# An expert loop turned round: rows stationary and weights moving for experts 1 to 14, with three of eight chunks of gate and up in f32r passes

## The chip, the cores and the metric

The kernel runs on one core of one Trainium2 chip. The metric is the device time of one execution in microseconds. What is compared is the median of several runs.

## The reference, cut to what matters

One inference step of a one-layer encoder: 512 prompt rows and 64 sample rows of width 1024, first mixed (pooling and differential attention), then sent through a mixture of 16 experts of which each row uses two, then normalized. The part around the change is the mixture and the last norm:

```python
combine = jnp.sum(jax.nn.one_hot(expert_id, N_EXPERTS, dtype=jnp.float32) * top_w[..., None], axis=2)
moe = jnp.zeros((B, T, D_MODEL), jnp.float32)
for e in range(N_EXPERTS):
    he = jax.nn.silu(h2 @ w_gate[e]) * (h2 @ w_up[e])
    moe = moe + combine[..., e:e + 1] * (he @ w_down[e]).astype(jnp.float32)
x = x + moe.astype(x.dtype)
...
y_prompt = rmsnorm(xp, g_final)
y_sample = rmsnorm(xs, g_final)
```

Here h2 is T x 1024, w_gate and w_up are 1024 x 256 for each expert, and w_down is 256 x 1024. All data are float32.

## The kernel before, in words

Every engine has its own program, written out in order, and the engines meet at semaphores. Nothing reorders the work: what stands behind a waiting instruction on its engine waits too.

After the attention and the router, the loop over the 16 experts begins (the stages of the profile from 246 us on). Each expert has 128 slots for rows. The stage of expert i on TensorE is the function `expert` (line 1251): `gate_up` (line 1197) multiplies w_gate and w_up (stationary, eight chunks of 128 rows, two halves of 128 columns each) with the transposed rows xT (moving, 128 columns), 32 products in f32, each of which the profile lists as two matmul instructions. Then `transpose_rows` turns the next expert's gathered rows, `slot_lists` makes the lists of rows for expert i+3, and `down_split` (line 1212) makes the down product of expert i-1 in three f32r passes: each f32 operand is split into a high part (he_hi, w_hi) and a low part (he_lo, w_lo), and high x high, high x low and low x high are summed. Since the hidden values come out of gate and up transposed already, they go straight into the down product.

In an iteration i ScalarE (lines 1590 to 1640) takes the square sum of a finished row block (`square_sum`, from i = 6 on), then `silu(i)`, then eight copies with a scale of the next expert's transposed rows from PSUM to xT (`rows_out`), then `wd_his(i+1)`: the two casts that make the high part of the next expert's w_down. VectorE (lines 2136 to 2230) makes he, he again and its low part (`he_out`), the lists (`lists_out`), a one-hot matrix, the norm of a finished row block (`finish_row`, from i = 6 on), the accumulation of expert i-1's result (`add_rows`), and the low part of w_down (`wd_los`).

The weights of an expert are three loads of 1 MB (w_gate, w_up, w_down) that SyncE issues into a ring of four slots, all with one semaphore a slot (`ring_loaded`, 48 when the three are there). The gate and up loads of expert i+4 go out when gate and up of expert i are done. The w_down load of expert i+3 goes out when the down product of expert i-1 is done, that is at the end of stage i, and when a gather of rows has landed (line 560). GpSimd issues, for each expert, the gather of its h2 rows (line 702), the gather of their sums so far, the store of sums, and from expert 6 on the two stores of finished rows (line 707). The store of sums waits for the accumulation.

Of the kernel before, what the change touches and what calls it, by code (L numbers as in the profile page):

```python
# [34 lines left out]
P = 128  # L35
# [26 lines left out]
RING = 4  # L62
NOWHERE = 1024
# [24 lines left out]
def build(nc, x_prompt, x_sample, cache_k, cache_v, state_pool, g_mix, w_in, w_pool, pool_scale,  # L88
# [4 lines left out]
    with ctx:  # L93
# [65 lines left out]
        region_v = sb("region_v", [P, 3584])  # L159
# [30 lines left out]
        def wd_hi(i):  # L190
            return wd_hi_last if isinstance(i, int) and i == E - 1 else wd_hi_two[:, i % 2]
        wd_lo = [r.rearrange("p (c n) -> p c n", c=FC) for r in
# [18 lines left out]
        hT_pair = w_hi_extra[:, :].rearrange("p (k b t) -> p k b t", k=KC, b=2)  # L211
        w_out_hi = [region_p_r[:, 0:D], region_p_r[:, D:2 * D], region_x_r[:, 0:D], region_x_r[:, D:2 * D], ring0_r[:, 4096:5120], ring0_r[:, 5120:6144],
# [94 lines left out]
        gsub_loaded = sem("gsub_loaded")  # L307
# [14 lines left out]
        gfin_loaded = sem("gfin_loaded")  # L322
# [22 lines left out]
        hist_full = sem("hist_full")  # L345
        hist_evac = sem("hist_evac")
        lam_dots = sem("lam_dots")
        lam_exp = sem("lam_exp")
        lam_made = sem("lam_made")
# [42 lines left out]
        early_onehot = sem("early_onehot")  # L392
        oh_last_ready = sem("oh_last_ready")
# [10 lines left out]
        he_lo_ready = sem("he_lo_ready")  # L404
        wd_hi_ready = sem("wd_hi_ready")
# [15 lines left out]
        ov_w_free = sem("ov_w_free")  # L421
        ov_gather_begun = sem("ov_gather_begun")
# [9 lines left out]
        last_bias = sem("last_bias")  # L432
# [22 lines left out]
        def _(sp):  # L455
# [51 lines left out]
            sp.dma_start(gsub[:, :], g_subln.rearrange("a (v o) -> (a v) o", o=1)).then_inc(gsub_loaded, 16)  # L507
# [47 lines left out]
            for i in range(E - RING):  # L555
# [6 lines left out]
                if i == 2:  # L562
                    sp.wait_ge(routed, 1)
                    sp.dma_start(gfin, g_final.rearrange("(a d) -> a d", a=1).to_broadcast([P, D])).then_inc(gfin_loaded, 16)
# [5 lines left out]
            with sp.If(n_ov > 0):  # L570
                with sp.Fori(0, MAXOV) as j:
                    with sp.If(j < n_ov):
                        e = sp.value_load(ctl[0:1, DS(j, 1)], min_val=0, max_val=E - 1)
                        load_expert(RING - 1, e, ov_w_loaded)
                        sp.wait_ge(ov_down_done, j + 1)
                        sp.sem_inc(ov_w_free, 1)
# [11 lines left out]
        def _(pool):  # L588
# [50 lines left out]
            pool.wait_ge(lam_made, 1)  # L639
# [107 lines left out]

            gather_first()
# [11 lines left out]
            for i in range(E):  # L760
# [10 lines left out]
                if 1 <= i < E - 1:  # L771
                    gather_acc(i + 1)

# [10 lines left out]
            with pool.If(n_ov > 0):  # L784
# [8 lines left out]
                with pool.Fori(0, MAXOV) as j:  # L793
                    with pool.If(j < n_ov):
                        pool.wait_ge(ov_idx_ready, j + 1)
                        pool.sem_inc(ov_gather_begun, 1)
# [3 lines left out]
                        pool.sem_inc(ov_gather_begun, 1)  # L800
                        store_acc(0, ov_stored)
                        pool.wait_ge(ov_final, j + 1)
                        pool.sem_inc(ov_gather_begun, 1)
# [9 lines left out]
        def _(pe):  # L813
# [124 lines left out]
            ins.then_inc(hist_full, 1)  # L938
# [8 lines left out]
            pe.wait_ge(hist_evac, 1)  # L947
# [212 lines left out]
            pe.wait_ge(early_onehot, 1)  # L1160
# [51 lines left out]
            def down_split(u, i, bank):  # L1212

                b, w_hi = u % 2, wd_hi(i if isinstance(i, int) else u)
                for half in range(2):
# [8 lines left out]
                    ins.then_inc(down_done, 1)  # L1224

            def first_rows():
# [6 lines left out]
                pe.wait_ge(oh_last_ready, 1)  # L1233
# [17 lines left out]
            def expert(it, u, left):  # L1251
# [5 lines left out]
                def lists_of(n):  # L1257
                    pe.wait_ge(onehot_ready, i + n + 1)
                    pe.wait_ge(idx_ready, i + n + EARLY + (1 if first and n == 0 else 0))
                    slot_lists((u + n) % RING * EPG + it + (u + n) // RING, (u + n) % RING)  # L1260
# [3 lines left out]
                pe.wait_ge(xT_act, i + 1)  # L1264
                pe.wait_ge(ring_loaded[u], it * 48 + 48)
                gate_up(u, b, up_full)
# [12 lines left out]
                if not first and left != 0:  # L1279
                    if isinstance(it, int) and i == 1:  # L1280
                        pe.wait_ge(state_evac, 1)
                    pe.wait_ge(he_ready, i)
                    if not (isinstance(it, int) and i == 1):
                        pe.wait_ge(added, i - 1)
                    pe.wait_ge(wd_lo_ready, i)
                    down_split((u - 1) % RING, i - 1, 4)
                if left == 1:
                    pe.wait_ge(idx_ready, E + EARLY + 1)
                    pe.wait_ge(he_ready, i + 1)
# [22 lines left out]
            pe.wait_ge(xT_act, E)  # L1312
# [20 lines left out]
        def _(act):  # L1333
# [88 lines left out]
            act.wait_ge(lam_dots, 1)  # L1422
# [184 lines left out]

            act.wait_ge(h2T_dve, NT)
            wd_his(0)

# [11 lines left out]
            for i in range(E):  # L1622
# [5 lines left out]
                if i + 1 < E:  # L1628
                    act.wait_ge(xg_transposed, i + 2)
                    for k in range(4 if i == 0 else 0, KC):  # L1630
# [710 lines left out]
```

## Time and profile before

| | |
|---|---|
| median of 3 runs | 435.69 us (435.27 to 435.9) |
| the profiled execution | 435.72 us, its span 433.6 us |
| mean granted clock of TensorE | 0.994 of full speed |
| TensorE busy | 413.9 us, 95% of the span |
| VectorE busy | 273.2 us, 63% |
| ScalarE busy | 197.8 us, 46% |
| GpSimd busy | 126.3 us, 29% |
| stages of experts 8 to 12 | 10.98 to 11.0 us each |

The span is the stretch from the first to the last instruction; the time of an execution is some 2.1 us longer. A matmul instruction is listed with the time from its start to its modelled end, so neighbours overlap: what a product costs in a stream is read from start to start, or from the chain, where its pieces stand end to end.

### The profile page before, as it was taken

The numbers are of one execution on the slowest core, as the hardware profiler recorded it, in microseconds if no ns is written. First come the engines' busy times: TensorE is split into PE (matmuls) and PEld (weight loads), VectorE is DVE, ScalarE is ACT, GpSimd is POOL, SyncE is SP. The second block draws the span as 40 slices with busy tenths as digits, with TensorE's granted clock in tenths as the row PEclk, the third lists the DMA queues.
The fourth block names the chain that finished last, engine by engine and source line by source line (L and its number), as shares of the span: only waits on it lengthen the run. The fifth ranks groups of instructions, "written<-read, shape, count | busy, mean of one in ns | idle before, by whom it ended". The sixth has DMA issues, their size and how long they took to land.

```text
span 433.6 us, 7776 instructions
## 1 busy us (share of the span) xinstructions
PE 413.9 (95%) x2919; PEld 364.1 (84%) x2919; DVE 273.2 (63%) x655; ACT 197.8 (46%) x485; POOL 126.3 (29%) x209
## 2 busy tenths in 40 slices
PE   6899999999999999999999999999989999999991
PEld 3687999997876886788887799999989999999981
DVE  2756430805759898635346898755566777776974
ACT  5566230705565766332222734444544555555632
POOL 2012000200034325151000323333334555554443
PEclk9999999999999999999999999999999999999997
DMA  7951704406000049923223789899999989986121
GB/s 250 323 182 50 231 2 135 169 2 202 2 1 3 0 155 418 373 97 147 97 98 129 245 322 421 335 403 379 355 339 341 374 332 386 364 321 251 59 89 47
DMA packets 32073, 91.36 MB, mean 211 GB/s; under 512 B 11200, under 2 KB 11712, under 8 KB 27942
## 3 DMA queue, kind: packets, MB, share of 16 engines
q1 hardware_dynamic: 20790, 71.97, 44.4%
q0 software_dynamic: 11248, 18.93, 12.3%
q8 instruction: 21, 0.34, 0.4%
q14 instruction: 14, 0.11, 0.1%
HBM read 86.38 MB, written 26.01 MB: 259 GB/s over the span
## 4 chain that ended last, share of the span: by engine, by line
PE 78%; DMA 7%; DVE 6%; ACT 4%; issue 3%; POOL 0%; SPq 0%; DVEq 0%; ACTq 0%; POOLq 0%
PE ps L1201 23%; PE ps L829 10%; PE ps L831 9%; PE ps L830 9%; DMA region_w<-in_w_down 5%; PE ps L1218 3%; PE ps L1219 3%; PE ps L1223 3%; PE ps L1194 3%; PE ps L993 2%; PE ps L1135 2%; PE ps L958 2%; DMA region_x<-in_x_prompt 1%; PE ps L976 1%; PE ps L1122 1%
## 5 line engine op out<-in xcount | busy, mean ns | idle before, releaser
L1201 PEld LDWEIGHTS ps<-region_p,region_a 128*128 128x128 f32 x512 | 58.3, 192 | 1.0 <-DVE region_p L2042 0.4
L1201 PE MATMUL ps<-region_p,region_a 128*128 128x128 f32 x512 | 58.5, 275 | 0.0
L831 PE MATMUL ps<-region_a_r,region_w_r 128*128 128x288 f32 x192 | 56.5, 295 | 0.0
L829 PE MATMUL ps<-region_a_r,ring_r 128*128 128x288 f32 x128 | 40.6, 317 | 0.0
L830 PE MATMUL ps<-region_a_r,ring_r 128*128 128x288 f32 x128 | 37.7, 295 | 0.0
L831 PEld LDWEIGHTS ps<-region_a_r,region_w_r 128*128 128x128 f32 x192 | 36.0, 188 | 0.0
L1592 ACT ACTIVATE region_p<-ps,gffn_sb 128x128 f32<-128x128 f32 x116 | 31.6, 384 | 7.7 <-PE ps L1194 7.7
L1613 ACT ACTIVATE region_t<-ps 128x256 f32<-128x256 f32 x16 | 6.1, 384 | 57.8 <-PE ps L1201 57.8
L1201 PEld LDWEIGHTS ps<-region_p,region_w 128*128 128x128 f32 x256 | 29.1, 192 | 1.8 <-issue 1.6
L702 POOL DMA_INDIRECT region_x<-h_rows,lists x13 | 16.7, 1283 | 47.3 <-DVE slot_w L2145 47.3
L1201 PE MATMUL ps<-region_p,region_w 128*128 128x128 f32 x256 | 29.3, 275 | 1.2 <-DMA region_w<-in_w_down 1.2
L829 PEld LDWEIGHTS ps<-region_a_r,ring_r 128*128 128x128 f32 x128 | 24.1, 188 | 6.8 <-issue 3.3
L1201 PEld LDWEIGHTS ps<-region_p,ring 128*128 128x128 f32 x256 | 29.1, 192 | 0.8 <-DVE region_p L2064 0.5
L1201 PE MATMUL ps<-region_p,ring 128*128 128x128 f32 x256 | 29.3, 276 | 0.4 <-DVE region_p L2064 0.4
L2151 DVE TENSOR_TENSOR region_t_r<-region_t,ps 128x256 fp32r<-128x256 f32 x16 | 6.7, 418 | 33.7 <-ACT region_t L1613 33.7
L2168 DVE SCALAR_TENSOR_TENSOR mix<-ps,slot_w,mix 128x1024 f32<-128x1024 f32 x15 | 19.2, 1281 | 10.6 <-PE ps L1223 6.3
L1783 DVE TENSOR_SCALAR region_q<-ps 128x288 f32<-128x288 f32 x8 | 3.7, 457 | 34.0 <-PE ps L831 34.0
L830 PE MATMUL ps<-region_w_r,mix_r 128*128 128x512 f32 x64 | 25.0, 391 | 0.0
L1218 PE MATMUL ps<-region_q_r,region_t_r 128*128 128x512 f32 x60 | 24.7, 411 | 0.0
L830 PEld LDWEIGHTS ps<-region_a_r,ring_r 128*128 128x128 f32 x128 | 24.1, 188 | 0.0
L1453 ACT ACTIVATE region_p<-ps,negm 128x128 f32<-128x128 f32 (+4 forms) x40 | 20.8, 528 | 5.8 <-DVE negm L1815 5.8
L707 POOL DMA_INDIRECT out_y_prompt<-region_x,lists x12 | 12.0, 1004 | 34.1 <-DVE region_x L2184 31.0
(365 smaller groups left out, 1020.1 us busy)
## 6 DMA issues: line engine op xcount, KB each, us to landing
region_a<-in_w_gate SPq DMA_DIRECT2D x8, 1024.0 KB, 9.3
region_a<-in_w_up SPq DMA_DIRECT2D x8, 1024.0 KB, 17.5
region_a<-in_w_down SPq DMA_DIRECT2D x8, 1024.0 KB, 18.5
region_w<-in_w_in SPq DMA_DIRECT2D x2, 2048.0 KB, 10.1
region_w<-in_w_out SPq DMA_DIRECT2D x2, 2048.0 KB, 7.9
ring<-in_w_gate SPq DMA_DIRECT2D x4, 1024.0 KB, 8.6
ring<-in_w_up SPq DMA_DIRECT2D x4, 1024.0 KB, 17.2
ring<-in_w_down SPq DMA_DIRECT2D x4, 1024.0 KB, 13.2
```

The costliest lines, as they stand in the source:

```text
L702: pool.indirect_dma_start(out=dst, out_offset=None, in_=src, in_offset=bass.IndirectOffsetOnAxis(ap=at, axis=0), bounds_check=bound[n], oo ...
L829: pe.matmul(out, lhs_hi, rhs_hi, start=first, stop=False)
L830: pe.matmul(out, lhs_hi, rhs_lo, start=False, stop=False)
L831: return pe.matmul(out, lhs_lo, rhs_hi, start=False, stop=last)
L1194: ins = pe.transpose(ps[:, k // 4, (k % 4) * P:(k % 4 + 1) * P], src[:, k, :], ident[:, :])
L1201: ins = pe.matmul(ps[:, 2 + b, (first + c) * P:(first + c + 1) * P], w[:, k, c * P:(c + 1) * P], xT[:, b, k, :], start=(k == 0), stop=(k = ...
L1218: pe.matmul(ps[:, bank + half, :], he_hi[:, b, c, :], w_hi[:, c, n], start=(c == 0), stop=False)
L1219: pe.matmul(ps[:, bank + half, :], he_hi[:, b, c, :], wd_lo[u][:, c, n], start=False, stop=False)
L1223: ins = pe.matmul(ps[:, bank + half, :], he_lo[:, b, c, :], w_hi[:, c, n], start=False, stop=(c == FC - 1))
L1453: ins = act.activation(prob[0:m, n % 2, c, 0:w], ps[0:m, 2 * (n % 2) + c, 0:w], ACT.Exp, bias=negm[0:m, n % 2, c:c + 1], scale=-1.0, accum ...
L1592: return act.activation(xT[:, b, k, :], ps[:, k // 4, (k % 4) * P:(k % 4 + 1) * P], ACT.Copy, scale=gffn_sb[:, k:k + 1])
L2168: dve.scalar_tensor_tensor(acc, ps[:, bank:bank + 2, :], slot_w[:, w:w + 1], acc, ALU.mult, ALU.add).then_inc(added, 1)
```

## The change

For experts 1 to 14 the rows become the stationary operand of gate and up, and the weights of w_gate and w_up (256 columns side by side) the moving one (`gate_up_mixed`). Five of the eight chunks stay in f32, ten products. The other three are made in three f32r passes, 18 products, for which both operands are split: the high parts of the rows come from ScalarE (`rows_hi`) and their low parts from VectorE (`rows_lo`); the high parts of the first three chunks of both weights come from ScalarE (`gu_his`, two tiles of 768 columns) and the low parts from VectorE (`gu_los`). The hidden values now come out with the rows on the partitions, so TensorE transposes them (`transpose_he`, two transposes between the halves of the down product of the expert before), and ScalarE and VectorE read the high and low parts from PSUM. GpSimd takes over one of the two halves of the low part of w_down for experts 1 to 13 (`wd_lo_half`). With POOL_FROM at 768, GpSimd has no part of the other subtraction. The one-hot matrix moves behind the norm of a finished row block on VectorE, the overflow counts two iterations later, and the load of the final gain two experts later. Some semaphores are merged.

```diff
+NF = 3
+POOL_FROM = 768
...
+            def gate_up_mixed(slot, b, i, signal):
+
+                hi, lo = wgu_hi[slot % 2], wgu_lo[slot]
+                for a in range(2):
+                    out = ps[:, 2 + b, a * FE:(a + 1) * FE]
+                    for k in range(NF, KC):
+                        pe.matmul(out, xT[:, b, k, :], wgu_sb[slot][:, a, k], start=(k == NF), stop=False)
+                    if a == 0:
+                        pe.wait_ge(xlo_ready, i)
+                        pe.wait_ge(gu_lo_ready, i)
...
+                    for k in range(NF):
+                        f = slice(k * FE, (k + 1) * FE)
+                        ins = three_passes(out, xT_hi[:, b, k, :], xT_lo[:, b, k, :], hi[a][:, f], lo[a][:, f], False, k == NF - 1)
+                ins.then_inc(signal, 1)
...
+            def transpose_he(u, i):
+
+                pe.wait_ge(he_ready, i + 1)
+                for c in range(FC):
+                    ins = pe.transpose(ps[:, 6 + u % 2, FE + c * P:FE + (c + 1) * P], he_tok[:, u % 2, c * P:(c + 1) * P], ident[:, :])
+                ins.then_inc(heT_full, 1)
...
+            def gu_his(i):
+
+                act.wait_ge(ring_loaded[i % RING], 48 * (i // RING + 1))
+                if i >= 2:
+                    act.wait_ge(up_full, i - 1)
+                for a in range(2):
+                    act.copy(wgu_hi[i % 2][a], wgu_part[i % RING][a]).then_inc(gu_hi_ready, 1)
...
+            def rows_hi(i):
+
+                b = i % 2
+                for k in range(NF, 4):
+                    rows_out(b, k)
+                for k in range(NF):
+                    ins = act.activation(xT_hi[:, b, k, :], ps[:, 0, k * P:(k + 1) * P], ACT.Copy, scale=gffn_sb[:, k:k + 1])
+                ins.then_inc(xhi_ready, 1)
...
+                    if mixed(i):
+                        he_hi_out(i)
                     if i < E - 2:
                         wd_his(i + 1)
                     if i == E - 3:
                         wd_his(E - 1)
+                    if mixed(i + 2):
+                        gu_his(i + 2)
...
+            def rows_lo(i):
+
+                b = i % 2
+                dve.wait_ge(xhi_ready, i)
+                for k in range(NF):
+                    ins = dve.scalar_tensor_tensor(xT_lo[:, b, k, :], ps[:, 0, k * P:(k + 1) * P], gffn_sb[:, k:k + 1],
+                                                   xT_hi[:, b, k, :].bitcast(F32), ALU.mult, ALU.subtract)
+                ins.then_inc(xlo_ready, 1)
...
+            def wd_lo_half(i):
+
+                pool.wait_ge(wd_hi_ready, FC * i + 2)
+                pool.tensor_tensor(wd_lo[i % RING][:, 1, :], wd_sb[i % RING][:, 1, :], wd_hi(i)[:, 1, :].bitcast(F32),
+                                   ALU.subtract).then_inc(lo_by_pool, 1)
...
                 elif i + EARLY < E:
                     lists_out(i + EARLY)
+                if i >= 1 and mixed(i + 1):
+                    rows_lo(i + 1)
+                if mixed(i):
+                    he_lo_out(i)
+                if i > RING + 1:
+                    finish_row(i - 2)
                 if i + EARLY + 1 < E:
                     expert_onehot(i + EARLY + 1)
-                if i > RING + 1:
-                    finish_row(i - 2)
                 if i >= 1:
                     add_rows(i - 1)
                 if i < E - 2:
                     wd_los(i + 1)
                 if i == E - 3:
                     wd_los(E - 1)
+                if mixed(i + 2):
+                    gu_los(i + 2)
```

On ScalarE, the order of one iteration before (the one in which expert 11's silu, L1613, is made and expert 12's w_down is cast from `ring`):

```order
L1619 ACTIVATE region_q,ssq<-mix 128x1024
L1613 ACTIVATE region_t<-ps 128x256
L1592 ACTIVATE region_p<-ps,gffn_sb 128x128 x8
L1606 CAST region_q_r<-ring 128x1024 x2
L1619 ACTIVATE region_q,ssq<-mix 128x1024
```

The same iteration of the change (L1713 is the square sum, L1707 the silu, L1694 the high parts of the rows, L1699 the high part of he, L1683 the high parts of gate and up):

```order
L1713 ACTIVATE region_q,ssq<-mix 128x1024
L1707 ACTIVATE region_t<-ps 128x256
L1661 ACTIVATE region_p<-ps,gffn_sb 128x128
L1694 ACTIVATE region_p_r<-ps,gffn_sb 128x128 x3
L1661 ACTIVATE region_p<-ps,gffn_sb 128x128 x4
L1699 CAST region_t_r<-ps 128x256
L1675 CAST region_q_r<-ring 128x1024 x2
L1683 CAST region_w_r<-region_a 128x768 x2
L1713 ACTIVATE region_q,ssq<-mix 128x1024
```

The two casts of 768 columns read the slot (`region_a`) of expert 13, two experts on, and stand ahead of the next square sum and silu.

On TensorE, the end of gate and up and the down product before (expert 12's stage; L1201 is gate and up, L1194 the transposes of rows, L1218 to L1223 the down product's passes):

```order
L1201 MATMUL ps<-region_p,ring 128x128 x32
L1194 MATMUL ps<-ident,region_x 128x128 x8
L1188 MATMUL ps<-region_q,region_v 128x8 x5
L1218 MATMUL ps<-region_q_r,region_t_r 128x512
L1219 MATMUL ps<-region_w_r,region_t_r 128x512
```

The change at the stage of expert 13: one f32 group and the first f32r products (L1246 is f32, L857 to L859 the three passes):

```order
L1246 MATMUL ps<-region_a,region_p 128x256 x5
L857 MATMUL ps<-region_w_r,region_p_r 128x256
L858 MATMUL ps<-region_a_r,region_p_r 128x256
L859 MATMUL ps<-region_w_r,w_hi_extra 128x256
L857 MATMUL ps<-region_w_r,region_p_r 128x256
```

One group of five f32 products and nine f32r products is made for gate, and one for up. Behind the first half of the down product two transposes (L1261) are new.

## Rows read from the trace of the kernel before

**Rows 1.** The page, busy time and the chain's shares by engine
```profile
PE 413.9 (95%) x2919; PEld 364.1 (84%) x2919; DVE 273.2 (63%) x655; ACT 197.8 (46%) x485; POOL 126.3 (29%) x209
...
PE 78%; DMA 7%; DVE 6%; ACT 4%; issue 3%; POOL 0%; SPq 0%; DVEq 0%; ACTq 0%; POOLq 0%
```
**Rows 2.** Chain of waits, expert 7's weights, then expert 10's stage: start, us, what
```profile
300.06 23.00 DMA region_w<-in_w_down
...
356.37 7.14 PE ps L1201 x64
363.51 0.87 PE ps L1194 x8
...
366.89 0.45 PE ps L1223 x2
```
**Rows 3.** Windows, stages of experts 1, 6, 10, 14: busy, clock, DMA share, GB/s
```profile
255.64:267.07 11.43, 11.43 (x102) 10.94 (x102) 9.59 (x37) 4.30 (x11) 2.32 (x2) 1.00 1.01 408
...
311.04:323.20 12.16, 10.95 (x89) 10.12 (x89) 7.82 (x19) 5.71 (x14) 4.10 (x3) 1.00 0.94 345
...
356.37:367.35 10.98, 10.98 (x91) 10.47 (x91) 8.27 (x19) 5.71 (x13) 5.97 (x5) 1.00 0.97 385
...
400.18:411.84 11.66, 11.66 (x89) 11.03 (x89) 10.63 (x19) 7.50 (x15) 4.62 (x3) 1.00 0.22 70
```
**Rows 4.** Issues of w_down (experts 7, 8, 14), and their us to landing
```profile
300.06 0.38 SPq L485 DMA_DIRECT2D region_w<-in_w_down  x1
...
311.04 0.38 SPq L485 DMA_DIRECT2D ring<-in_w_down  x1
...
383.76 0.38 SPq L485 DMA_DIRECT2D region_a<-in_w_down  x1
...
region_w<-in_w_down SPq DMA_DIRECT2D x1, 1024.0 KB, 23.0
...
ring<-in_w_down SPq DMA_DIRECT2D x1, 1024.0 KB, 22.1
...
region_a<-in_w_down SPq DMA_DIRECT2D x1, 1024.0 KB, 11.1
```
**Rows 5.** Chain: f32 products of 288 columns; timeline: f32r ones, first and last
```profile
171.18 0.97 PE ps L1029 x4
...
49.72 0.29 PE L829 MATMUL ps<-region_a_r,ring_r 128*128 128x288 f32 x1
...
53.95 0.30 PE L831 MATMUL ps<-region_a_r,region_w_r 128*128 128x288 f32 x1
```
**Rows 6.** ScalarE's groups from 334.4 to 367.4, three iterations
```profile
L1592 ACT ACTIVATE region_p<-ps,gffn_sb 128x128 f32<-128x128 f32 x24 | 6.5, 385 | 1.5 <-PE ps L1194 1.5
L1606 ACT CAST region_q_r<-region_a 128x1024 fp32r<-128x1024 f32 x4 | 4.0, 1044 | 1.7 <-PE ps L1223 1.7
L1619 ACT ACTIVATE region_q<-mix 128x1024 f32<-128x1024 f32 x3 | 3.2, 1057 | 2.7 <-DVE mix L2168 2.7
```
**Rows 7.** VectorE's groups of the same stretch; GpSimd's 1024-wide memset of the span
```profile
L2158 DVE TENSOR_TENSOR region_a_r<-region_a,region_q_r 128x1024 fp32r<-128x1024 f32 x4 | 4.7, 1218 | 0.0
...
L2151 DVE TENSOR_TENSOR region_t_r<-region_t,ps 128x256 fp32r<-128x256 f32 x3 | 1.3, 421 | 7.2 <-ACT region_t L1613 7.2
...
L678 POOL MEMSET region_x<- 128x1024 f32 x1 | 1.3, 1268 | 0.0
```
**Rows 8.** Late gathers: issues, us to landing, and VectorE's wait
```profile
373.88 1.03 POOL L702 DMA_INDIRECT mix<-summed_rows,lists  x1 [0.30 <-issue]
...
376.63 1.34 POOL L702 DMA_INDIRECT region_x<-h_rows,lists  x1 [1.73 <-DVE slot_w L2145]
...
mix<-summed_rows,lists POOLq DMA_INDIRECT x1, 19.7
...
region_x<-h_rows,lists POOLq DMA_INDIRECT x1, 19.7
...
393.68 1.28 DVE L2168 SCALAR_TENSOR_TENSOR mix<-ps,slot_w,mix 128x1024 f32<-128x1024 f32 x1 [3.21 <-DMA mix<-summed_rows,lists]
```

More of the change, by code:

```diff
@@ L404, in build @@
         he_lo_ready = sem("he_lo_ready")
+        heT_full = sem("heT_full")
+        heT_hi = sem("heT_hi")
+        gu_hi_ready = sem("gu_hi_ready")
+        gu_lo_ready = sem("gu_lo_ready")
+        lo_by_pool = sem("lo_by_pool")
+        xhi_ready = sem("xhi_ready")
+        xlo_ready = sem("xlo_ready")
         wd_hi_ready = sem("wd_hi_ready")
@@ L772, in _ @@
                     gather_acc(i + 1)
+                if 1 <= i + 1 <= E - 3:
+                    wd_lo_half(i + 1)
+                if POOL_FROM < NF * FE and 3 <= i + 2 < E - 1:
+                    gu_lo_part(i + 2)
             pool.wait_ge(routed, 1)
@@ L946, in _ @@
             pe.wait_ge(ktok_evac, NT)
[L947 removed]
+            pe.wait_ge(ktok_evac, NT + 1)
             def scores(n):
@@ L1224, in down_split @@
                     ins.then_inc(down_done, 1)
+                    if half == 0 and between is not None:
+                        between()
             def first_rows():
@@ L1259, in lists_of @@
                     pe.wait_ge(idx_ready, i + n + EARLY + (1 if first and n == 0 else 0))
+                    if n == EARLY and not (isinstance(it, int) and i <= 1):
+                        pe.wait_ge(he_lo_ready, i)
                     slot_lists((u + n) % RING * EPG + it + (u + n) // RING, (u + n) % RING)
@@ L1263, in expert @@
                     pe.wait_ge(xT_dve, i + 1)
-                pe.wait_ge(xT_act, i + 1)
+                pe.wait_ge(xT_act, i + 1 if first else i)
                 pe.wait_ge(ring_loaded[u], it * 48 + 48)
-                gate_up(u, b, up_full)
+                if isinstance(it, int) and i == 1:
+                    pe.wait_ge(xhi_ready, 1)
+                if first or left == 0:
+                    gate_up(u, b, up_full)
+                else:
+                    gate_up_mixed(u, b, i, up_full)
                 if isinstance(it, int) and i == 1:
@@ L1629, in _ @@
                     act.wait_ge(xg_transposed, i + 2)
-                    for k in range(4 if i == 0 else 0, KC):
-                        ins = rows_out((i + 1) % 2, k)
-                    ins.then_inc(xT_act, 1)
+                    if mixed(i + 1):
+                        rows_hi(i + 1)
+                    if i >= 1:
+                        for k in range(4 if mixed(i + 1) else 0, KC):
+                            ins = rows_out((i + 1) % 2, k)
+                        ins.then_inc(xT_act, 1)
+                    if mixed(i):
+                        he_hi_out(i)
                     if i < E - 2:
```

138 lines of the change are left out of this document (91 added, 47 removed).

## The prediction

> **What bounds the kernel now.** I read the page first: TensorE is busy for 413.9 of 433.6 us and holds 78% of the chain that ended last [rows 1]. A reader would stop there and count matmuls. The stages say more. In the chain of waits, a stage of one expert takes 10.98 us (from 356.37 to 367.35): 7.14 for the gate and up product, then 3.84 for eight transposes, the lists and twelve down products [rows 2]. But in the same rows one stage waits for a weight load: w_down, issued at 300.06, arrives 23.00 later. So I read the stages' windows and the loads. The DMA share is 1.01, 0.94 and 0.97 in three stages of the loop, and 0.22 in expert 14's [rows 3]. And w_down of expert 7 is issued at 300.06 and lands 23.0 later, at 323.06; that of expert 8 goes out at 311.04, 12 us before, and lands at 333.14; that of expert 14 goes out at 383.76 and lands at 394.86 [rows 4]. Each is issued before its forerunner has landed, so the queue never runs dry: six experts' loads land in 394.86-333.14 = 61.7 us, 10.29 each, at the pace of the transfers and not at that of TensorE. Call this D. TensorE's 10.98 is longer, which is why it waits once only: the loads gain 0.7 us a stage on it.
>
> **The change, part by part.** I write S(i) for the start of expert i's stage and measure from the profiled execution: span 433.6, time 435.72, which is 0.03 from the median 435.69.
>
> *Gate and up.* Removed: 32 f32 products of 128 columns, 7.14 us. Added: 10 f32 products of 256 columns. The four instructions of two f32 products of 288 columns take 0.97 [rows 5], 0.485 a product, or 0.431 at 256: 4.31. And 18 f32r products of 256 columns: 33 of 288 columns start from 49.72 to 53.95 [rows 5], 0.132 each, so 0.117 at 256: 2.11. Sum 6.42, less 0.72. A denser pace from fewer columns could be eaten by weight loading for every product; but there is a load for every product now too, 2919 and 2919 [rows 1], so I take the sum (bounds 6.2, and 6.7 with f32r left at 0.132). Added too: two transposes at 0.87/8 = 0.11 [rows 2], 0.22. The rest of a stage becomes 4.06. Net 0.50 a stage, P = 10.48. If TensorE decided all 14 stages: -7.0 us.
>
> *The high parts of the weights.* ScalarE now casts two tiles of 768 for expert j in the iteration of j-2, and it waits there for all three loads of j; before, the first use was the cast of w_down at the end of j-1's stage. These casts stand ahead of the square sum and of the silu of j-1 on the same queue. Prices: 1024 wide is 1.00 (4.0 for 4), so 2 x 0.75 = 1.50; the square is 1.06 plus its 0.19 read, 1.25; a silu is like 0.38, eight row copies take 6.5/3 = 2.2 [rows 6]. The silu of j-1 can start at S(j-1)+6.42. How late may it be? The down products take 0.45 for two [rows 2], so their second half starts 1.37 before the stage's end, at 2.47 after gate and up, and he must be there: silu 0.38, product 0.42 [rows 7], hand-overs about 0.2, so 1.4 us of slack; by the row copies 4.06-0.4-2.2 = 1.4 as well; VectorE leaves about 1.0 (below). I take 1.2. So the loads of j must have landed by S(j-1)+6.42+1.2-1.25-1.50 = S(j-1)+4.9. Before it was S(j-1)+10.98 or so: 6 us later.
>
> *What the loads then allow.* The final gain (0.5 MB, about 1.7 us at D for 3 MB) moves behind expert 7's loads, so they land at 321.4 and S(6) >= 316.5; TensorE alone would have been there at 311.04-5x0.50 = 308.5, plus up to 2 for stage 1, where the two subtractions (2x0.92) stand behind expert 0's work: swallowed by this wait. S(7) >= 333.14-4.9 = 328.2, against 323.2 before. By then fewer gathers have used the queue: moved are 385 GB/s x 10.98 = 4.2 MB a stage [rows 3] of which weights are 3.15, so a quarter is gathers and stores; the landing now falls 0.45 of a stage earlier in that work, 0.45 x 0.25 x 10.29 = 1.2; I take 1.0: S(7) = 327.2. From there P (10.48) is over D (10.29), and TensorE decides: S(14) = 327.2+7x10.48 = 400.6, against 400.18: **+0.4**.
>
> *VectorE and the order of its work.* Busy 8.27 in the stage of expert 10 [rows 3]. Less one product of 256 (0.42) and one subtraction of 1024 (1.18, from 4.7 for 4), plus three 128-wide low parts (0.22 to 0.42 each, I take 0.25) and two subtractions of 768 (0.92): 9.3 of 10.48. It is still covered, but in a queue: the low part of he can't start before 3.65 after gate and up (8 row copies and a cast on ScalarE stand ahead), and 8.3 us follow it, the norm of a finished row (3.0), the one-hot (0.8), the accumulation (1.2), 1.2 and 1.8. It ends 1.5 into the next expert, where 2.0 is what TensorE allows. So an accumulation ends at 9.0 after gate and up, where before it was 6.7, and GpSimd's store and gather of sums behind it go out about 1 us later. Behind them GpSimd gets half of the w_down subtraction: nearest rows a 1024-wide memset 1.27 [rows 7] and two such operands at most twice that, 1.3 to 2.5. The gather of h2 rows behind it goes out about 1 us later. One-hots behind the norm cost nothing by themselves.
>
> *The gathers.* They were on the edge already: the sums for expert 11, whose gather was issued at 373.88, land 19.7 later, and VectorE waited 3.21 for them, covered then; the h2 rows for expert 14, issued at 376.63, landed 19.7 later, at 396.3 [rows 8], and were wanted at the end of gate and up of expert 13, 367.35+2x10.98+7.14 = 396.45. Now two stages are 1.0 shorter and the issue is 1.0 later: 1.9 late on TensorE, and VectorE's wait is no longer covered, at about the same place. I take **+1.8** once (bounds 0 and 4). Stage 14: -0.50, and +0.5 for VectorE's low parts of the last two w_down, which are not halved: 0.
>
> Sum 0.4+1.8+0 = **+2.2**, so 435.72+2.2 = 437.9.
>
> [...] The stage of expert 10 moved 385 GB/s, and that of expert 1 408 [rows 3]. [...]
>
> **Rivals.**
> - *Forecast*, loads and gathers cost more than TensorE gains: +1 to +4.5. 0.42.
> - *Loads are no limit*: the queue serves faster when asked earlier, TensorE decides. For it: DMA share 0.94 and 0.97, not 1, in two of the stages. Against: the landings above. 14x0.50 less 1.5 for stage 1: -5.5, 430.2. This ends on the other side. 0.12.
> - *The two sides cancel*: weights land 2 us earlier, or the gathers still fit. 435 to 436.5, 436.0. 0.30, a third of it more than 0.2% faster.
> - *VectorE becomes the bound*: its subtractions read two tiles from SBUF, and GpSimd's subtraction runs beside them. From 0.5 us of extra a stage it decides. With 1.27 lost a stage, 0.8 over eight stages: +6, 442. [...] 0.16.
>
> **How the numbers follow.** What a measurement of this kernel can tell is 0.2%, 0.9 us. Faster: 0.12+0.10 = 0.22. Same: 0.20. Slower: 0.42+0.16 = 0.58. The range leaves out the first rival and the tail of the last: 433.0 to 443.0. The forecast's own range is 436.7 to 440.2.
>
> **What would show it.** Right: gate and up in 6.3 to 6.6 us; quiet stages of 10.5; TensorE waiting around experts 5 to 7, with ScalarE's casts of 768 ended by a w_down load; expert 7's loads landing at 320 to 323 in spite of earlier stages; stage 14 starting at 401 to 404; a late wait for gathered rows. Wrong: weights that land 3 us or more earlier (then I am 3 to 7 too high); gate and up at 6.9 or more; stages over 11 with VectorE without idle time (then too low).

## The result and the profile after

| | before | after |
|---|---|---|
| median of 4 runs each | 435.79 us (435.27 to 436.96) | 445.63 us (445.54 to 447.16) |
| ratio, 95% interval | 1 | 1.0219 [1.0187, 1.0251] |
| span of the profiled execution | 433.6 us | 443.7 us |
| granted clock of TensorE | 0.994 | 0.990 |

The change costs 2.2%, about 9.5 us (the interval excludes 1, and not 1.02). The direction was forecast; the size, 437.9 us in a range up to 443, was not. All ratios, here and below, leave out the few executions in which the granted clock stood far lower (0.65 to 0.85 on average, 462 us and more). They are those on record, each against the kernel before on its chip, and differ somewhat from the quotients of the medians: for e1 below, 1.0106 beside 440.78/437.25 = 1.0081. The first rows of the page of the changed kernel answer to [rows 1]: busy time, the chain's shares by engine, and one group of instructions (count, busy us, mean ns, idle time before).

```profile
PE 412.0 (93%) x2583; PEld 350.5 (79%) x2583; DVE 309.2 (70%) x698; ACT 221.8 (50%) x527; POOL 162.8 (37%) x222
...
PE 53%; DVE 27%; issue 6%; DMA 6%; ACT 6%; POOL 0%; SPq 0%; DVEq 0%; ACTq 0%; POOLq 0%
...
L2311 DVE SCALAR_TENSOR_TENSOR root<-root 128x1 f32<-128x1 f32 x33 | 22.7, 688 | 1.2
```

TensorE lost hardly any busy time, and the chain moved from TensorE (78% before, 53% now) to VectorE (6%, now 27%). The group is the strangest row of the page: an operation on one element in each partition takes 688 ns on average. TensorE's own part came out as worked out. The chain of waits in the stage of expert 6:

```profile
317.26 2.16 PE ps L1246 x10
319.42 0.12 PE ps L857
...
320.49 2.16 PE ps L1246 x10
...
323.72 0.87 PE ps L1222 x8
...
326.18 0.22 PE ps L1261 x2
...
327.79 0.86 PE ps L1246 x4
```

Ten f32 instructions (five products) take 2.16 us, an f32r product 0.12; gate and up take 323.72-317.26 = 6.46, and a stage with nothing in its way 327.79-317.26 = 10.53. The forecast had 6.42 and 10.48. The windows of two such stages and of two late ones answer to [rows 3] (length, busy us of PE, PEld, DVE, ACT, POOL with counts, clock, DMA share, GB/s):

```profile
263.62:274.18 10.56, 10.56 (x71) 9.48 (x68) 7.39 (x16) 6.21 (x14) 8.09 (x6) 1.00 0.87 347
317.26:327.79 10.53, 10.53 (x67) 9.44 (x66) 6.86 (x15) 7.33 (x16) 6.73 (x4) 1.00 0.94 361
355.65:367.49 11.84, 10.74 (x67) 9.36 (x66) 11.56 (x23) 7.32 (x16) 9.21 (x7) 1.00 0.91 328
404.10:414.10 10.00, 9.47 (x53) 8.13 (x52) 9.56 (x19) 6.69 (x15) 6.37 (x5) 1.00 0.18 49
```

The late stage takes 11.84, and VectorE is busy for 11.56 of it. The timeline there shows why (start, us, engine, line):

```profile
361.01 2.58 DVE L2311 SCALAR_TENSOR_TENSOR root<-root 128x1 f32<-128x1 f32 x1
361.19 2.38 POOL L762 TENSOR_TENSOR region_a_r<-region_a,region_q_r 128x1024 fp32r<-128x1024 f32 x1
...
363.83 0.22 DVE L2311 SCALAR_TENSOR_TENSOR root<-root 128x1 f32<-128x1 f32 x1
```

VectorE's tiny operation with two inputs from SBUF takes 0.22 us when it is alone and 2.58 when it meets GpSimd's subtraction, and it ends 0.02 after it. VectorE stands still for 2.36 us, nearly the whole of GpSimd's 2.38. It happens again at 372.85, 384.67, 396.49 and 407.57 (and before, at 349.18), 2.57 to 2.59 each time.

The second place is the stage of expert 3. The chain of waits there:

```profile
264.44 9.01 DMA region_x<-h_rows,lists
273.51 8.93 DMA ring<-in_w_down
282.46 0.84 ACT region_v_r L1683
283.32 4.21 DVE ring_r L2281 x2
...
290.97 0.25 DVE region_k L2220
291.25 0.43 DVE region_t L2253
```

The gather of h2 rows holds SyncE until 273.5, w_down of expert 4 goes out behind it and lands at 282.4, and the casts of its gate and up wait for it. Then the two subtractions take 4.21 where two alone take 1.83 (again beside GpSimd), and the overflow count, which the change put here, follows until 291.2 before VectorE comes to the hidden values for which TensorE waits. TensorE stands for 4.4 us, until 291.72. Something comes on top that no line of the chain names: toward the end of that stop the granted clock of TensorE goes down to 0.50 and stays there for 3.35 us. The windows of that stretch and of the whole interval:

```profile
291.22:294.57 3.35, 2.85 (x8) 2.37 (x9) 2.56 (x8) 0.37 (x1) 1.01 (x1) 0.50 0.73 300
284.69:301.17 16.48, 12.06 (x67) 10.43 (x66) 14.35 (x33) 6.39 (x14) 6.52 (x5) 0.90 0.83 322
```

TensorE works for 2.85 of these 3.35 us, at half its pace (down products 0.43 from start to start, where those before the stop have 0.23), so some 1.4 us are lost. The 5.95 us by which this interval is over the 10.53 of a quiet one therefore part into 2.38 beside GpSimd (4.21 less 1.83), 1.4 at half clock, and 2.2 for the late load and the count; e1 below, without the other two, has 1.9 for these. In the next interval (11.86) GpSimd meets the placing of the overflow: an operation of 0.24 takes 2.62. Here are the intervals between the ends of gate and up of neighbouring experts, read in each trace from the start of the eight transposes of rows behind them. "Tail" is the rest of the span after expert 14.

| kernel | 1 | 2 | 3 | 4 | 5 to 7 | 8 | 9 to 13, sum | 14 (last) | sum of 14 | tail |
|---|---|---|---|---|---|---|---|---|---|---|
| before | 9.79 | 10.98 | 10.98 | 11.01 | 10.97, 10.98, 12.43 | 10.97 | 54.95 | 10.82 | 153.88 | 26.44 |
| after | 10.76 | 10.56 | 10.51 | 16.48 | 11.86, 10.52, 10.53 | 10.53 | 58.36 | 11.07 | 161.18 | 29.66 |
| e1 | 10.76 | 10.56 | 10.53 | 12.40 | 10.51, 10.52, 10.53 | 13.23 | 55.85 | 10.32 | 155.21 | 27.85 |
| e5 | 10.76 | 10.56 | 10.51 | 11.71 | 10.54, 10.52, 10.53 | 10.86 | 58.85 | 10.51 | 155.35 | 27.75 |
| e6 | 10.76 | 15.54 | 10.50 | 10.51 | 10.54, 10.53, 10.53 | 13.04 | 55.88 | 10.32 | 158.15 | 27.84 |
| e9 | 10.75 | 10.57 | 10.53 | 11.68 | 10.53, 10.52, 10.53 | 10.86 | 53.37 | 10.33 | 149.67 | 27.82 |
| e10 | 9.79 | 11.04 | 10.97 | 11.01 | 10.98, 10.98, 10.98 | 10.98 | 54.90 | 10.75 | 152.38 | 26.38 |
| e11 | 10.75 | 10.56 | 10.54 | 15.15 | 11.51, 10.53, 10.52 | 10.53 | 58.37 | 11.09 | 159.55 | 29.65 |

Interval k ends with gate and up of expert k, so a wait in the second part of expert 3's stage stands in column 4, and one in expert 7's in column 8. Each row is one profiled execution. Some of them hold stretches at half clock, which other executions of the same kernel may lack: 1.4 to 1.7 us lost in column 4 of the change and of e11, in column 2 of e6, and in the interval 13 of e5 (12.16, mean clock 0.86). The loops of before and e1 ran at 1.00 throughout.

### The profile page after: what moved, and what is told of

The parts are those of the page before. It is cut to its first block, busy times and chain, and to the rows that moved or that the text cites. A ratio compares the mean times of both kernels' runs of the same rounds, so it can differ in the third digit from the quotient of the medians.

```text
span 443.7 us, 7253 instructions
## 1 busy us (share of the span) xinstructions
PE 412.0 (93%) x2583; PEld 350.5 (79%) x2583; DVE 309.2 (70%) x698; ACT 221.8 (50%) x527; POOL 162.8 (37%) x222
## 4 chain that ended last, share of the span: by engine, by line
PE 53%; DVE 27%; issue 6%; DMA 6%; ACT 6%; POOL 0%; SPq 0%; DVEq 0%; ACTq 0%; POOLq 0%
PE ps L857 10%; PE ps L859 9%; PE ps L858 9%; DVE root L2311 5%; PE ps L1246 3%; DVE region_a_r L2281 2%; DVE mix L2301 2%; PE ps L1021 2%; DMA region_x<-h_rows,lists 2%; DMA ring<-in_w_down 2%; PE ps L1163 2%; PE ps L1229 2%; PE ps L986 2%; DMA region_x<-in_x_prompt 1%; DVE ring_r L2281 1%
## 5 line engine op out<-in xcount | busy, mean ns | idle before, releaser
L859 PE MATMUL ps<-region_a_r,region_w_r 128*128 128x288 f32 x192 | 56.6, 295 | 0.0
L857 PE MATMUL ps<-region_a_r,ring_r 128*128 128x288 f32 x128 | 40.6, 317 | 0.0
L1246 PE MATMUL ps<-region_a,region_p 128*128 128x256 f32 x160 | 37.2, 380 | 0.0
L859 PEld LDWEIGHTS ps<-region_a_r,region_w_r 128*128 128x128 f32 x192 | 36.1, 188 | 0.0
L1246 PEld LDWEIGHTS ps<-region_a,region_p 128*128 128x128 f32 x160 | 29.8, 190 | 4.3 <-DVE region_p L2143 0.5
L857 PEld LDWEIGHTS ps<-region_a_r,ring_r 128*128 128x128 f32 x128 | 24.1, 188 | 6.8 <-issue 3.3
L1713 ACT ACTIVATE region_q<-mix 128x1024 f32<-128x1024 f32 x11 | 11.7, 1060 | 27.5 <-DVE mix L2301 27.5
L1661 ACT ACTIVATE region_p<-ps,gffn_sb 128x128 f32<-128x128 f32 x74 | 22.4, 391 | 4.2 <-PE ps L1222 4.2
L718 POOL DMA_INDIRECT summed_rows<-mix,lists x12 | 18.0, 1503 | 15.3 <-DVE mix L2301 13.2
L2311 DVE SCALAR_TENSOR_TENSOR root<-root 128x1 f32<-128x1 f32 x33 | 22.7, 688 | 1.2
L713 POOL DMA_INDIRECT region_x<-h_rows,lists x13 | 13.6, 1046 | 24.8 <-DVE slot_w L2246 23.3
L1617 ACT ACTIVATE region_v<-region_q 128x512 f32<-128x512 f32 (+1 forms) x10 | 6.3, 627 | 32.0 <-DVE region_q L2023 21.8
L718 POOL DMA_INDIRECT out_y_sample<-region_x,lists x12 | 19.1, 1589 | 3.7 <-issue 3.7
L2023 DVE TENSOR_TENSOR region_q<-ps,region_q 128x512 f32<-128x512 f32 (+1 forms) x10 | 6.8, 685 | 18.8 <-PE ps L859 18.2
```

What stands on the lines that cost most here:

```text
L713: pool.indirect_dma_start(out=dst, out_offset=None, in_=src, in_offset=bass.IndirectOffsetOnAxis(ap=at, axis=0), bounds_check=bound[n], oo ...
L718: pool.indirect_dma_start(out=dst, out_offset=bass.IndirectOffsetOnAxis(ap=at, axis=0), in_=src, in_offset=None, bounds_check=bound[n], oo ...
L857: pe.matmul(out, lhs_hi, rhs_hi, start=first, stop=False)
L859: return pe.matmul(out, lhs_lo, rhs_hi, start=False, stop=last)
L1246: pe.matmul(out, xT[:, b, k, :], wgu_sb[slot][:, a, k], start=(k == NF), stop=False)
L1661: return act.activation(xT[:, b, k, :], ps[:, k // 4, (k % 4) * P:(k % 4 + 1) * P], ACT.Copy, scale=gffn_sb[:, k:k + 1])
```

## The experiments

Theory A is the stop: GpSimd's subtraction (2.38) holds VectorE's operations with two inputs from SBUF, and VectorE then sets the stage. Theory B is the forecast's: loads and gathers take back what TensorE gains. The rivals to both are the moved overflow count and the order of the one-hot.

**e1, VectorE makes both halves.**

```diff
-                if 1 <= i + 1 <= E - 3:
-                    wd_lo_half(i + 1)
...
-                for c in range(1 if by_pool(i) else FC):
+                for c in range(FC):
```

> The change with one part undone: VectorE makes both halves of w_down's low part, GpSimd none. Theory P (ports): GpSimd's two-operand subtraction of 2.38 us keeps VectorE from reading two SBUF tiles as long as it runs; without it a late stage is VectorE's 9.5 us of work plus 1.15, so 10.6 to 10.8 where it was 11.83, and the hits of 2.1 to 2.4 at experts 3 and 4 go: 432 to 436. Theory W (work): VectorE simply has too much work since the change; 1.15 more per expert makes stages of 12.9 and 452 or more. Theory G (loads): the weights bind; 442 to 446 as now.

Measured: 440.78 us, ratio 1.0106 [1.0058, 1.0153]. Half of the loss or more goes, though VectorE has more work. The profiled execution is the fastest of the six, 437.04: it and one of 438.13 have a mean clock of 0.994, and the other four, at 0.983 to 0.986, take 440.4 to 442.4. So this row of the table shows the kernel at a higher clock than most of its executions have. The waits of the forecast stand in its chain, the first for w_down of expert 8, the second for gathered rows:

```profile
311.26 18.35 DMA ring<-in_w_down
...
367.23 19.29 DMA region_x<-h_rows,lists
```

**e2, nobody makes the second half** (TensorE reads the high part in its place, so one low term of the product is another number).

```diff
-                        pe.matmul(... he_hi[:, b, c, :], wd_lo[u][:, c, n], ...)
+                        pe.matmul(... he_hi[:, b, c, :], wd_lo[u][:, c, n] if c == 0 else w_hi[:, c, n], ...)
```

> Left out: the second half of w_down's low part is made by nobody; the pass that read it reads the high part again, so TensorE's work is the same and the low term of half of w_down is missing. Theory P: stages are TensorE's 10.5 throughout; with no load wait 445.6 less 1.3 in 7 late stages, less 5 around experts 3 and 4: 430 to 432. Theory G: with TensorE early at experts 5 to 7 the wait for loads that I forecast comes back, up to 5 us: 434 to 437, with ScalarE's casts of 768 ended by w_down. Theory W: as P here, since the work is less.

Measured: 439.52 us, 1.0059 [1.0027, 1.0091]. The interval overlaps e1's: 1.2 us less of VectorE's work a stage is worth about 2 us in all by the two ratios, and perhaps nothing. The same two waits are there, of 17.50 and 20.19. Interval 4 takes 14.70, 1.4 of it lost at half clock, though GpSimd has no part in it.

**e3, GpSimd fills with zeros instead of subtracting** (operands of the product as in e2).

```diff
-                pool.tensor_tensor(wd_lo[i % RING][:, 1, :], wd_sb[i % RING][:, 1, :], ..., ALU.subtract)
+                step(pool.memset(wd_sb[i % RING][:, 1, :], 0.0))
+                pool.memset(wd_sb[i % RING][:, 1, :], 0.0)
```

> As the run without the half, but GpSimd writes zeros twice over the 1024 columns in the place of its subtraction (about 2.5 us of writing, no reading; the low term is missing as there). If it is the read side that the two engines share, VectorE's root operations stay at 0.22 us and the time is that of the run without the half within 1.5 us. If any GpSimd access to SBUF blocks VectorE, one operation of 2.5 us stays in each late iteration and the time is 441 to 446.

Measured: 438.56 us in a single run. The timeline beside the fills, where VectorE subtracts two tiles from SBUF:

```profile
283.76 0.97 POOL L762 MEMSET region_w<- 128x1024 f32 x1
284.12 1.83 DVE L2281 TENSOR_TENSOR ring_r<-ring,region_v_r 128x768 fp32r<-128x768 f32 x2 [2.58 <-ACT region_v_r L1683]
284.79 0.95 POOL L763 MEMSET region_w<- 128x1024 f32 x1
```

Two subtractions take the 1.83 that they take alone, and the interval of expert 10 is 10.52, where the change has 11.84. The two fills, 0.97 and 0.95, only write and don't stop VectorE here, so it isn't GpSimd's time that costs; that it is its reading is what e8 tests.

**e4, two chunks in f32r instead of three**, both halves on VectorE (NF = 2).

```diff
-NF = 3
-POOL_FROM = 768
+NF = 2
+POOL_FROM = 512
```

> Two of eight chunks in f32r instead of three, and VectorE makes both halves of w_down's low part. TensorE: 12 f32 products at 0.216x2 and 12 f32r at 0.12, 6.6 us instead of 6.45, stages 10.7. VectorE: 0.8 us less an expert than with three chunks, so 9.8. Theory P: TensorE-bound, 432 to 435, equal to or a little under the run with three chunks and both halves on VectorE. Theory W: 447 or more. Theory G: ScalarE's casts are shorter by 0.5, 434 to 440.

Measured: 440.95 us, 1.0078 [1.0042, 1.0114], which e1's interval holds. Quiet stages of 10.66 instead of 10.53 make no difference that can be told: TensorE's pace is not what decides. Interval 4 takes 16.18 here, with no subtraction on GpSimd: w_down of expert 4 takes 11.69 us from issue to landing (e1: 8.30), and 1.7 us of the interval are lost at half clock. A long interval 4 doesn't need the stop.

**e5, w_down with semaphores of its own.** The casts of gate and up then wait only for gate and up.

```diff
             def load_down(slot, e, signal=None):
-                signal = signal or ring_loaded[slot]
+                signal = signal or w_v_loaded[slot]
...
-                act.wait_ge(ring_loaded[i % RING], 48 * (i // RING + 1))
+                act.wait_ge(ring_loaded[i % RING], 32 * (i // RING + 1))
```

> VectorE makes both halves of the low part of w_down (as in e1), and w_down has semaphores of its own, so that ScalarE's casts of w_gate and w_up of expert j wait only for those two loads, not for w_down of j, which is then wanted a stage later. If the wait of experts 7 and 8 is the forecast's (casts of j need w_down of j by S(j-1)+4.9), the stage of 13.2 us around expert 7 falls to about 10.6 and the ratio falls from e1's 1.011 by 0.006 to about 1.005, the late wait for gathered rows staying. If instead the queue is full and only moves the wait to the next late load, the 2.7 us come back a stage later as a wait for w_gate or w_up and the ratio stays at 1.011.

Measured: 438.75 us, 1.0051 [1.0027, 1.0075]. The wait for w_down goes (column 8 of the table: 13.23 to 10.86). But part of it comes back: columns 9 to 13 grow from 55.85 to 58.85, and the sum of the 14 is 155.35 against 155.21. About half of that growth is not a transfer: interval 13 (12.16, e1 10.57) has TensorE busy throughout, at half clock from 388.6 to 392.0. Without it e5 would be some 1.5 us ahead of e1's profiled execution. The two ratios' intervals overlap from 1.0058 to 1.0075, so what the edit is worth stays open between nothing and 0.5%. The waits of TensorE and VectorE from 355 to 400:

```profile
DVE mix L2294 <- DMA mix<-summed_rows,lists: 4.7, 3, 2.3
...
PE ps L1220 <- DMA region_x<-h_rows,lists: 3.2, 2, 1.9
```

A part of the wait that is taken away at one transfer stands at the next ones. Whether the amount of bytes is the limit, and not one late load, is what e9 and e10 test.

**e6, the overflow count back at iterations 0 and 1**, otherwise e1.

```diff
-                if i == 2:
+                if i == 0:
                     incl = count_overflow()
-                if i == 3:
+                if i == 1:
```

> e1 with the overflow count and its placing back at iterations 0 and 1 of VectorE. If the moved count causes the long stage of expert 3 (12.4 in e1, 16.5 in the changed kernel), that stage falls to 10.5 and the loop gains 1.9 us, ratio 1.006, perhaps with a longer stage of expert 1 or 2 in its place. If the long stage comes from the gather that holds w_down of expert 4 on SyncE, it stays at 12 or more.

Measured: 441.4 us, 1.0109 [1.0063, 1.0156], as e1. The stage of 12.40 falls to 10.51, and an earlier one grows to 15.54, 1.5 of it lost at half clock: the count stands in VectorE's queue ahead of what TensorE needs at either place. Moving it is not a cause of the loss against its old place.

**e7, the one-hot ahead of the norm again**, nothing else undone.

```diff
+                if i + EARLY + 1 < E:
+                    expert_onehot(i + EARLY + 1)
                 if i > RING + 1:
                     finish_row(i - 2)
-                if i + EARLY + 1 < E:
-                    expert_onehot(i + EARLY + 1)
```

> The changed kernel with the one-hot matrix back ahead of the norm of a finished row, nothing else. The order is not a price by itself: the prediction has it at nothing, ratio 1.022 as before. If the order matters because GpSimd's subtraction meets another instruction of VectorE, the stages of 11.8 us from expert 9 on change by up to 1 us each, either way. 1.012 to 1.032.

Measured: 449.9 us, 1.0291 [1.0232, 1.0351], slower still by the stages below; the ratio's interval overlaps the change's up to 1.0251. The timeline:

```profile
362.35 3.68 DVE L2136 TENSOR_TENSOR region_v<-iota_one,rm 128x640 bf16<-128x640 f32 x1
362.95 2.38 POOL L762 TENSOR_TENSOR region_a_r<-region_a,region_q_r 128x1024 fp32r<-128x1024 f32 x1
365.50 1.43 POOL L713 DMA_INDIRECT region_x<-h_rows,lists  x1 [0.16 <-issue]
365.95 0.14 DVE L2307 TENSOR_SCALAR root<-ssq 128x1 f32<-128x1 f32 x1
```

The one-hot, 0.82 us alone, now takes 3.68. Here it is the one-hot, first behind the hidden values and with two tiles to read, that meets the subtraction; before the norm's first two-input operation there are three with one input (0.14, 0.14 and 0.15 in the change, also where they run beside the subtraction, from 337.96 to 338.35), and this order loses them. The stages go from 11.83 to 12.33. So the edit to the order, priced at nothing, saves 0.5 us a stage as long as GpSimd subtracts.

**e8, GpSimd copies** (one input, one output; products as in e2).

```diff
-                pool.tensor_tensor(wd_lo[i % RING][:, 1, :], wd_sb[i % RING][:, 1, :], ..., ALU.subtract)
+                pool.tensor_copy(wd_lo[i % RING][:, 1, :], wd_sb[i % RING][:, 1, :])
```

> GpSimd copies half of w_down (one input, one output) where the changed kernel has it subtract (two inputs); TensorE reads the copy's place only as before for c = 0 and w_hi for the other half, so the low part of that half is missing from the product. If only a GpSimd operation with two inputs shuts out VectorE, its tiny operations of two inputs stay at 0.22 us beside the copy and stages are 10.5; if every GpSimd read does, one of them again takes as long as the copy (1 to 1.5 us) in each stage from expert 9 on.

Measured: 440.73 us in a single run, intervals of 10.51 to 10.53 from expert 5 to 10, where the change has 11.84 in the last, then waits for gathers (11.42, 11.18, 12.66). Interval 4 is the longest of all, 17.49: w_down of expert 4 keeps the casts waiting until 284.69, and 2.8 us are lost at half clock (mean clock 0.80). The copy (283.66 to 284.72) meets nothing of VectorE in it. At one place the copy does meet a two-input operation (0.24 alone):

```profile
299.42 1.27 DVE L2225 TENSOR_TENSOR region_k<-region_k 128x80 f32<-128x80 f32 x1
299.54 1.04 POOL L762 CAST ring_r<-ring 128x1024 fp32r<-128x1024 f32 x1
```

So in this place a copy, which reads one tile, is enough to stop VectorE, for about its 1.04 (1.27 instead of 0.24). In the later stages the copy is over, or all but over, before the two-input operation comes up, behind operations that read PSUM (0.42) or one tile (0.14 to 0.15), and costs 0.05 at most (0.27 for 0.22, at 348.82). The expectation had the two apart the wrong way: the copy blocks, and the stages are 10.5 all the same.

**e9, e10, e11, a quarter of the weight bytes left out** in e1, in the kernel before and in the changed one: from expert 4 on, the last three chunks of gate and up keep an earlier expert's weights.

```diff
-                load_gate_up(i % RING, expert_at(i + RING))
+                load_part(i % RING, expert_at(i + RING))
...
+                for at, src in ((0, wg_v), (WB, wu_v)):
+                    sp.dma_start(ring[slot][:, at:at + 5 * FE], src[DS(e, 1), :, 0:5 * FE]...)
```

> e1 (VectorE makes both halves) with less traffic: in the loop five of eight chunks of w_gate and w_up are loaded and the last three keep an earlier expert's weights, so a quarter of the weight bytes is left out from expert 4 on. If the DMA queues' pace eats what TensorE gained, the waits for w_down of expert 8 and for the gathered rows go, all stages from expert 4 on take 10.5 and the time falls by 4 to 6 us against e1, ratio 0.993 to 0.998, faster than before. If the waits of e1 come from the order of the issues and not from the bytes, they stay within 1 us and the ratio is 1.005 to 1.010.

> The kernel before with the same quarter of the weight bytes left out. TensorE's 10.98 us a stage should hide all loads, so only its one wait (w_down of expert 7, 1.4 us) goes: ratio 0.996 to 1.000. If it gains 3 us or more, the loads cost the kernel before as well, in a way the profile did not show.

> The changed kernel with the same quarter of the weight bytes left out. If GpSimd's subtraction shuts out VectorE for its 2.4 us whatever the traffic, the stages from expert 9 on stay at 11.8 and only the long stage of expert 3 can shorten: ratio 1.008 to 1.020, at least 5 us above e9. If the price of the subtraction came from late data, the stages fall to 10.5 and the ratio is e9's.

| ratio to before | all bytes | a quarter less |
|---|---|---|
| before | 1 | 0.9970 [0.9951, 0.9989] |
| both halves on VectorE | 1.0106 [1.0058, 1.0153] | 0.9894 [0.9869, 0.9919] |
| the change | 1.0219 [1.0187, 1.0251] | 1.0163 [1.0135, 1.0191] |

The three of the right column ran on one chip. The kernel before gains 0.3%: its one wait of 1.4 us goes (12.43 to 10.98), and little more. The variant with both halves on VectorE gains 2.1% and is faster than the kernel before by 1.1%; its late stages are 10.6 to 10.8, at a DMA share of 0.90. It beats the lower end of its expectation. The changed kernel keeps its 11.84. Windows of a late stage, of e9 and then of e11:

```profile
362.20:372.80 10.60, 10.60 (x68) 9.35 (x67) 10.18 (x24) 7.43 (x16) 6.87 (x6) 1.00 0.90 305
```

```profile
353.33:365.17 11.84, 10.75 (x68) 9.36 (x67) 11.56 (x23) 7.33 (x16) 9.21 (x7) 1.00 0.84 283
```

With more subtracting to do, VectorE is busy for 10.18 in e9, and with less for 11.56 in e11. The stage keeps its 11.84 with a quarter fewer weight bytes, so the transfers don't set it. In expert 3's stage of e11 the count itself meets the subtraction (0.18 alone):

```profile
280.61 1.83 DVE ring_r L2285 x2
...
282.77 3.03 DVE region_k L2210
```

**e12, the hidden values of expert 15 ahead of the last norm**, otherwise e5.

```diff
             finish(E - 3, final_ready)
+            he_out(E - 1)
             dve.wait_ge(squared, E - 1 - RING)
             inverse_root(E - 2, step)
-            he_out(E - 1)
             finish(E - 2, final_ready)
```

> e5 (VectorE makes both halves, w_down with semaphores of its own) with the hidden values of expert 15 made on VectorE ahead of the norm of the row block of expert 14. In e5 the down product of the last expert starts 0.66 us late behind that norm. If VectorE's queue sets the tail, 0.5 to 0.7 us are gained on e5, ratio 1.003 to 1.004; if not, 1.005 as e5.

Measured: 440.05 us, 1.0086 [1.0053, 1.0119], a miss: no gain on e5, whose interval it overlaps. The tail is 28.87 in its profile against 27.75: the norm now stands ahead of the last sum instead, and ScalarE waits 3.4 us for that sum, where it waited 2.2.

## Why the prediction was wrong, point by point

- **Gate and up, the stage's length** (6.42 and 10.48): measured 6.46 and 10.53. Right.
- **"It is still covered"** is the step that failed. VectorE's own work was estimated well: 9.3, and 11.84-2.36 = 9.48 in the trace, where it runs without a gap. But the sum counted GpSimd's subtraction as GpSimd's time only (1.3 to 2.5 us, measured 2.38). It is VectorE's time too, as soon as an operation with two SBUF inputs comes up (2.58 for one of 0.22). 9.48+2.36 is 1.3 more than TensorE's 10.53, and e1, e3, e9 and e11 bear this out. This is the rival "VectorE becomes the bound", which stood at 0.16 with 1.27 a stage for its price, the price of a memset, [rows 7]. At that price alone VectorE would need 9.48+1.27 = 10.75 and lose 0.2 a stage. e3 shows that a memset is the wrong row for this: its fills of 0.97 and 0.95 don't read, and stop nobody. The rows of the trace before had no reading operation of GpSimd beside VectorE: that one stops the other was a supposition of this rival that no row showed, and the runs showed 2.36 us for a subtraction of 2.38.
- **Stage of expert 3.** Not foreseen. The forecast moved the overflow count without counting its 3.7 us where VectorE has least room. Of the 5.95 over a quiet interval 2.38 are the stop, 1.4 the half clock, and 2.2 the count behind a load that the gather holds back; that last part alone is 1.2 to 1.9 in e5 and e1, and over 3 in e4 and e8, where the casts wait longest for w_down of expert 4. e6 shows that the old place would cost more beside the new work.
- **TensorE's clock** has no term in the sum. The kernel before has a mean of 0.994, the change 0.990. Each low stretch in a profiled loop began in a wait of TensorE or within 2 us behind one (waits of 1.9 to 4.4 us), and most cost 1.4 to 1.7 us. But e1's loop passed waits of 1.6, 1.7 and 2.4 us at full clock. That the waits bring the clock down fits this and is not shown: no run put other work of TensorE in their place.
- **The loads** (wait around experts 5 to 8, S(14) at +0.4). Once GpSimd is quiet there is such a wait, for w_down of expert 8, 18.35 us from issue, with ScalarE's cast of 768 waiting. It costs TensorE 2.7 us in one stage, expert 7's; the forecast had 8 by the start of expert 6's (up to 2 of them given to stage 1) and nothing for stage 3. In the changed kernel itself it does not appear: when gate and up of expert 7 end, that loop is already 5.4 us behind e1's. P was sized right. For D, 10.29, e5 has 10.65 (w_down of experts 8 to 14 landing from 332.9 to 396.8), over P, though the last of them also went out late: "from there TensorE decides" was too hopeful. With all bytes e1's 14 intervals sum to 155.21, 1.3 more than before, and with a quarter less to 149.67.
- **The gathers** (+1.8). They come late, 19.3 to 21.5 us from issue, at the forecast's place. Their cost can't be parted from the loads': e5 turns a part of one into the other. Together the two cost e1 2.1% (e9 against e1, on two chips), about 9 us by the ratios, where the forecast's +2.2 against the -5.5 of its rival without a limit comes to 7.7.
- **Stage 14 and the tail at 0.** The tail is 1.4 us longer even in e9, where nothing else is late, and stage 1 0.96. VectorE's last norms and unhalved low parts stand in the tail, but what makes it longer is not shown; e12 moved one of them and gained nothing. TensorE's gain that arrives is therefore 0.9894 against 0.9970, 0.8% or 3.3 us, and not 7.
- **Luck.** e1's profiled execution, without the stop and at full clock, takes 437.04, and the forecast was 437.9. That doesn't bear the sum out: stage 3 and the tail stood at nothing and cost 3.3 us together, and the loads' wait was smaller than forecast.

The account of the 9.5 us, from the two columns of ratios, at 436 us for 1: TensorE's gain, with what VectorE and the tail take of it, -3.3; the bytes, +7.9 (9.2 in e1 less the 1.3 that they cost the kernel before); GpSimd's subtraction, +4.9 with all bytes. With fewer bytes the last is 11.7: the two causes cover each other, and neither alone is the answer. The half clock is inside these terms and not a fourth one. By their mean clocks most of e1's executions have it and most of e9's don't; taken at like clock (0.993 and over, 437.04 and 438.13 against 431.05 to 432.18, each beside its kernel before) the bytes come to about 6 us and not 9. By the quotients of the medians they are 7.5, and GpSimd's subtraction 6.3. So the sizes are good to 2 us at best, and some 3 us of what is put down to the bytes may be TensorE at half clock, if it is the waits that bring the clock down. No version that computes the reference beats the kernel before; e5 comes nearest.

## What to carry to other kernels

Before work is handed from VectorE to GpSimd, list VectorE's operations with two SBUF inputs: here a GpSimd subtraction of 2.38 us cost VectorE 2.36 as well, and VectorE had no slack as long as it, whatever the busy shares said. In e5, with quiet stages of 10.53 and loads of w_down that land 10.65 apart, one wait taken away (13.23 to 10.86) came back in part at the next transfers; to see whether bytes are the limit, leave some out and run both kernels so. When the profile's page gives a 0.2 us operation a mean of 0.7, it is worth a look at its longest instance. And before two profiled executions are compared stage by stage, read the granted clock of each stage: 16.48 and 12.40 (interval 4 of the change and of e1) differ by the stop and by a stretch at half clock, and only the first surely belongs to the edit.

## What the runs showed of the hardware that was not expected

- The stop doesn't scale with VectorE's operation: one element in each partition waits 2.36 us for a 2.38 us subtraction. A fill of GpSimd (0.97) stopped nothing in e3; a copy (1.04) held an operation of 0.24 for 1.27. VectorE's operations that read PSUM and one tile, or one tile alone, kept their time beside the subtraction: in the change 0.42 at 324.17 and 337.62, and 0.14, 0.14 and 0.15 from 337.96 on.
- In e7 the one-hot's row begins 0.60 before the subtraction's row, and it is the one that is stopped. GpSimd's row is then no sure mark of when VectorE is held; whether the operation was stopped midway or had not begun is open.
- TensorE stood for 4.4 us, and its granted clock was 0.50 from 291.22, 0.5 us before it went on, for 3.35 us (the change). In e5 a stop of 1.9 us (385.6 to 387.5) was followed by 3.4 us at 0.50, and in e1 one of 1.7 us at the same place in the program was not.
- Late gathers of at most 128 rows took 19.3 to 21.5 us from issue to landing (e1, e5), against 9.0 for the one issued at 264.4 (the change).
